# A hybrid decoder step on one core: quarters of weight units between page scores, part of a unit inside the turning of a table, norm sums in pairs

## What is computed

```python
h = rms_norm(x, g_mix)
q, k, v, u, gate_a, gate_s = split(h @ w_in)          # 1024 x 4096
q = rms_norm(q per head, g_q); k = rms_norm(k per head, g_k)
o = stick_breaking_attention(q, k, v)                  # samples also see 2 cached pages of 128 keys
y_ssm, h_last = s5_branch(u, ...)                      # 32 groups, 64 complex states each
ssm_out = (gelu(y_ssm) @ w_glu_val) * sigmoid(gelu(y_ssm) @ w_glu_gate)
x = x + (sigmoid(gate_a) * (o @ w_attn_out) + sigmoid(gate_s) * ssm_out) @ w_out
x = x + square(relu(rms_norm(x, g_mlp) @ w_up)) @ w_down
x = x + (p @ w_ple) * sigmoid(rms_norm(x, g_ple) @ w_ple_gate)
```

## Time and profile before

| | us |
|---|---|
| median of three runs | 948.61 |
| lowest, highest | 947.8, 949.62 |
| the profiled execution, whole | 947.96 |
| its span, first to last instruction | 946.2 |
| PE busy in the span | 922.9 (98%) |
| DVE busy | 610.8 (65%) |
| ACT busy | 439.5 (46%) |
| mean granted TensorE clock | 0.994 of full speed |

### The profile page before, as it was taken

How to read it: one execution, slowest core, us unless ns; L and a number is a source line. 1 busy time by engine, 2 the same in 40 slices (tenths; PEclk the granted TensorE clock), 3 DMA queues, 4 the chain that set the end, 5 groups by cost and what they waited for, 6 DMA issues and landing times.

```text
span 946.2 us, 17809 instructions
## 1 busy us (share of the span) xinstructions
PE 922.9 (98%) x7469; PEld 893.1 (94%) x7469; DVE 610.8 (65%) x855; ACT 439.5 (46%) x672; POOL 66.7 (7%) x115
## 2 busy tenths in 40 slices
PE   5999999999999999999999999999999999999998
PEld 4988999989999878999999999999999999999997
DVE  6399789821477845566567666666676666778453
ACT  7434333221677644445347344444444444445532
POOL 7000031300100310100000000000000000000000
PEclk9999999999999999999999999999999999999999
DMA  8422232822532748432322222322214322252203
GB/s 229 124 67 68 70 106 95 182 83 86 162 97 70 251 156 280 143 105 78 89 68 77 80 90 89 91 89 90 90 47 131 89 89 86 72 159 71 68 1 100
DMA packets 129991, 99.84 MB, mean 106 GB/s; under 512 B 14368, under 2 KB 120216, under 8 KB 129880
## 3 DMA queue, kind: packets, MB, share of 16 engines
q1 hardware_dynamic: 124392, 81.02, 29.1%
q0 software_dynamic: 5424, 17.65, 5.9%
q10 hardware_dynamic: 96, 0.04, 0.0%
HBM read 87.53 MB, written 11.03 MB: 104 GB/s over the span
## 4 chain that ended last, share of the span: by engine, by line
PE 88%; DVE 5%; ACT 4%; issue 2%; DMA 0%; ACTq 0%; DVEq 0%
PE dense L2228 61%; PE banks L2228 20%; PE banks L2381 3%; PE scoreA L2228 3%; PE scoreB L2228 1%; DVE Llo L1679 1%; ACT whi L1259 1%; DVE xtok L1805 1%; ACT t L1561 1%; DVE t L2053 1%; DVE Ssum L1655 0%; DVE mt L1729 0%; DMA xtok<-in_x_sample 0%; ACT ga L1601 0%; PE dense L2381 0%
## 5 line engine op out<-in xcount | busy, mean ns | idle before, releaser
L1679 DVE TENSOR_TENSOR wlo<-wraw,whi 128x1024 fp32r<-128x1024 f32 (+1 forms) x139 | 148.7, 1073 | 102.5 <-ACT whi L1259 90.0
L2228 PE MATMUL dense<-hid,whi 128*128 128x256 f32 (+1 forms) x1024 | 176.6, 294 | 0.1
L2228 PE MATMUL dense<-act_hi,whi 128*128 128x256 f32 (+1 forms) x736 | 169.7, 300 | 2.8 <-ACT act_hi L1413 1.4
L2228 PE MATMUL dense<-act_lo,whi 128*128 128x256 f32 (+1 forms) x736 | 165.7, 295 | 0.0
L2228 PE MATMUL dense<-act_hi,wlo 128*128 128x256 f32 (+1 forms) x736 | 165.4, 295 | 0.0
L2228 PEld LDWEIGHTS dense<-hid,whi 128*128 128x128 f32 x1024 | 152.4, 187 | 0.5 <-issue 0.5
L2228 PEld LDWEIGHTS dense<-act_hi,whi 128*128 128x128 f32 x736 | 125.0, 190 | 7.6 <-issue 3.9
L1259 ACT CAST whi<-wraw 128x1024 fp32r<-128x1024 f32 x100 | 104.9, 1050 | 45.7 <-PE banks L2228 43.8
L2228 PEld LDWEIGHTS dense<-act_lo,whi 128*128 128x128 f32 x736 | 125.9, 190 | 0.0
L2228 PEld LDWEIGHTS dense<-act_hi,wlo 128*128 128x128 f32 x736 | 125.4, 189 | 0.0
L2228 PE MATMUL dense<-hid,wlo 128*128 128x256 f32 (+1 forms) x512 | 108.8, 293 | 0.0
(11 more groups left out here) (368 smaller groups left out, 1574.5 us busy)
## 6 DMA issues: line engine op xcount, KB each, us to landing
wraw<-in_w_in SPq DMA_DIRECT2D x32, 512.0 KB, 4.1
wraw<-in_w_up SPq DMA_DIRECT2D x32, 512.0 KB, 4.1
wraw<-in_w_down SPq DMA_DIRECT2D x32, 512.0 KB, 3.9
gates_spill<-gst POOLq DMA_DIRECT2D x16, 288.0 KB, 2.6
page<-in_cache_k SPq DMA_DIRECT2D x16, 256.0 KB, 8.3
page<-in_cache_v SPq DMA_DIRECT2D x16, 256.0 KB, 7.6
wraw<-in_w_out SPq DMA_DIRECT2D x8, 512.0 KB, 3.7
wraw<-in_w_ple_gate SPq DMA_DIRECT2D x8, 512.0 KB, 3.6
```

The source lines that it names most:

```text
L1679: return nc.vector.tensor_tensor(out=lo, in0=whole, in1=f32(hi), op=ALU.subtract)
L2228: return nc.tensor.matmul(out, lhsT, rhs, start=start, stop=stop, skip_group_check=True)
```

## The change

Four edits, all in the schedule:

1. The norm sums are done two at a time: 0 and 1 after unit 2, 2 and 3 after unit 4, 4 and 5 after unit 6, 6 and 7 after unit 8. Before, one followed each of the units 1 to 8.
2. `turn_back`: between turns 1 and 2 of either table stands the first k step of the next unit (7, and 9): six matmuls, which that unit then no longer has to do.
3. The three half units between the page scores (34's second, both of 35) are cut into quarters of two k steps, 12 matmuls each. Pairs 0, 2 and 4 of pages, which had nothing between transposes and scores, get the first quarter, pairs 1, 3 and 5 the second. Split 37 moves with them, from pair 3 to pair 2.
4. Unit 57 is written as two halves with split 59 between them, where split 59 stood ahead of both.

```diff
+    def half_begin(k1):
+        if halves[0] == 0:
+            flush()
+        event("hpart", n[0], halves[0], k1)
+    def turn_back(part):
+        for i in range(4):
+            if i == 2:
+                event("part", n[0], 0, 1)
+                begun[n[0]] = 1
+            event("gt", part, i, place=2 + i % 2)
...
     unit()
     unit()
+    unit()
     event("qksum", 0)
-    unit()
     event("qksum", 1)
...
-    for i in range(4):
-        event("gt", 0, i, place=2 + i % 2)
+    turn_back(0)
...
-        if i in (1, 3, 5):
-            half_unit()
+        if i in (0, 2, 4):
+            half_begin(2)
+        elif i in (1, 3, 5):
+            half_unit(split_first=False)
...
     event("xsplit", 3)
     event("rscale", 3)
-    unit()
+    half_unit(split_first=False)
+    flush()
+    half_unit()
...
+                elif k == "hpart":
+                    begun[a[0], a[1]] = a[2]
+                    unit(a[0], [a[1]], k1=a[2])
                 elif k == "half":
-                    unit(a[0], [a[1]])
+                    unit(a[0], [a[1]], k0=begun.get((a[0], a[1]), 0))
```

More of the change, by code:

```diff
@@ L259, in schedule_of @@
     unit()
-    event("qksum", 2)
     event("s5in")
     unit()
+    event("qksum", 2)
     event("qksum", 3)
@@ L265, in schedule_of @@
     unit()
-    event("qksum", 4)
     event("s5sq")
     unit()
+    event("qksum", 4)
     event("qksum", 5)
-    for i in range(4):
-        event("gt", 0, i, place=2 + i % 2)
+    turn_back(0)
     event("s5g", 1)
     unit()
-    event("qksum", 6)
     event("s5c", 0)
     unit()
+    event("qksum", 6)
     event("qksum", 7)
-    for i in range(4):
-        event("gt", 1, i, place=2 + i % 2)
+    turn_back(1)
     event("s5c", 1, 0)
```

## The result

The changed kernel takes 940.5 us (median of 5 runs, 938.88 to 942.83), the kernel before, beside it on the same chip, 947.8 (5 runs, 944.8 to 949.62). The ratio is 0.9931, with an interval from 0.9909 to 0.9953.

What follows compares the result with a forecast made beforehand. PE, busy 98% of the span, was taken to bound the kernel. Early part 1.6, page quarters 1.9 and unit 57 1.1 sum to 4.6 us: 948.61 - 4.6 = 944.0 us, range 942.0 to 946.7.

Steps and rivals of the forecast that it cites:

- Sums in pairs: Norm sums after units 2 to 8: joining two visits saves 0.27 us, four times 1.1; bounds nothing to 3.2.
- Turning: Turning of both tables: six matmuls inside save 0.4 us each, 0.8 together; bounds 0.2 and 0.45 each.
- What takes some back: At the first norms PE, 1.9 us earlier, stands 0.2 to 0.4 us for DVE's `nrmr`, ready only some 0.65 earlier.
- the early part: Joined norm sums and table turnings, less PE's stand at the norms: 1.6 us saved, bounds 0.6 and 2.0.
- Quarters: Page scores: a quarter covers the copies in six pairs, 3.18 us each; 1.9 us saved, bounds 0 and 2.2.
- Unit 57: Before unit 58: the earlier addition removes PE's 0.98 us wait and some start-up; 1.1 us saved, bounds 0.9 and 1.2.
- (a): DVE sets the pace from the first norm on, the early part keeps 0.6 us: 945.0 us; chance 0.10.
- (b): Page scores: the quarter does not cover, or the slot's second visit waits for ACT; stage unchanged, 945.9 us; chance 0.03.
- (d): One more clock fall in another pass of y: 947.3 us, no change that could be told; chance 0.07.
- (e): Slower: all four passes of y, moved forward 1.6 us, meet a clock fall, 3.3 us each: 953.9 us; chance 0.04.
- The clock: Pass of y at 208 us: one fall costs 3.3 us; the change only moves the place forward by 1.6 us.
- rival (c): The clock fall at 208 us does not come, 3.3 us less: 940.7 us; chance 0.06.

Runs made afterwards that it cites:

- the third trace of before: The kernel before, unchanged, profiled once more; this run had no fall of the clock and took 945.17 us.
- edit 3 alone: The kernel before with only the quarters of half units between six pairs of pages: median 944.37 us, ratio 0.9982 (0.9964 to 1.0).

## Why the prediction was right in its edits and wrong in its time

**Sums in pairs: mechanism right, 1.1 where 1.36 was measured.** A single sum is 0.60 us from its start to the transposes behind it at 70.65:

```profile
70.05 0.67 PE L2228 MATMUL banks<-gst,hsum 128*16 128x288 f32 x4
```

Two are 1.08 (67.64 to 68.72). So the second costs 0.48, not 0.52, a joined visit saves 0.31 of the 0.79, and four save 1.24. The last 0.1 no row accounts for.

**Turning: mechanism right, 0.8 where 1.14 was measured.** I charged 0.18 us for the visit to dense matmuls and 0.85 for the transposes behind it. The rows of the changed kernel show 0.88 from 69.57 to 70.45, which is 0.09 beyond six matmuls, and 0.79 from 70.45 to 71.24. Two tables: 1.1 by the rows.

**What takes some back: right in kind, 0.3 forecast, 0.27 measured, in part by luck.** PE stands for DVE at the first norm and nowhere after it. But both sides of the meeting were mis-sized: PE came 2.61 earlier there, not 1.9, and DVE's `nrmr` was ready 1.2 earlier (101.02 to 99.81), not 0.65. With the forecast's 0.65 for DVE, PE's 2.61 would have left a stand of about 0.8. The two errors nearly cancel in the stand, in part because the same joined sums and the same turning move both engines. With this the early part gave 2.34 for 1.6, the largest of the mis-sized terms.

**Quarters: 1.9 forecast, 1.88 measured. Unit 57: 1.1 forecast, 1.13 measured.** No other engine had to give anything back, and PE's waits name no new transfer. Rivals (a) and (b) fall with these rows, and (d) and (e) with the clock: neither trace of the changed kernel has a fall in any pass of y.

**The clock is the step that failed.** The sum, 4.6, was set against a trace with a fall and a median of three runs, all of the upper group, and the result taken for a time that keeps the fall: "The change does not touch this place but moves it forward". That is true of the place, but the fall is no property of the kernel. By their times it came in 49 of 86 runs of before and in some 4 of 11 of the changed kernel. About half the runs have it, so the median lies in one group or the other, and the two medians of this result lie in different ones: 947.8 in the upper of before, 940.5 in the lower of after. Lower group against lower group the gain is 5.4 us (5.5 between the traces), and about 1.9 of the 7.3 is which runs made up the medians. Upper against upper it is 6.7 (medians 948.8 and 942.1), but from four runs of the changed kernel, none of them traced. Of the 3.5 us between forecast and result, 0.8 is the size of the edits (5.4 for 4.6), and the other 2.7 is the group: the forecast stood on 948.61, which is 3.5 above the lower group's median, and the result is a run of the lower group that lies 0.8 above its median. I had this as rival (c) with a time of 940.7, 0.2 from the result, and gave it 6 in 100. That it came so near is luck: its edits were 0.8 too small, and 940.5 is the highest run of a group whose median is 939.7. The Trainium skill ("TensorE: Matmul & The Clock Gate", What's actually happening) stood in the prediction with its statement that the chip's look at activity runs freely, and from it I concluded that both kernels meet falls alike. What the runs show is chance in each single run, which makes two groups and not a shared offset. Three runs within 1.8 us looked like a steady state; that three runs all fall in the upper group happens about once in five times (49/86 to the third power).

Whether the changed kernel meets the fall less often (4 of 11 against 49 of 86) can't be told from 11 runs. That its upper runs have their fall at this place was not traced, but it is supported: with the stand taken away in either way, none of its 12 runs lies above 939.6.

**A version that beats both** comes out of the search for the cause: the four edits with the last states out of the way, 938.85 (behind the unit) or 938.93 (bank 2). Against the median of the changed kernel's lower group (939.7) that is 0.8 us less (the stand's 1.24, read in the kernel before, would have given more; where the other 0.4 went stays open), and it has no upper group. It did not run in one comparison with the changed kernel, and the intervals of the ratios overlap (0.9905 to 0.9952 and 0.9887 to 0.993), so this rests on the groups and on the wait that is gone. Against before it is clear, by 0.8 to 0.9% of the time (ratios 0.9909 and 0.9923).

## What to carry over

When runs of a kernel differ by several tenths of a per cent, look at the single times before the median: two groups with nothing between point to an event that comes or not, and a forecast has to say in which group its base and its result lie. A short stand of PE beside small matmuls cost more than its length here: a wait of 0.8 us cost 1.24, and another 3.0 or 4.5 in about half the runs. Such a stand can go without moving any work, by a bank that the next step doesn't write.

## What the runs showed of the hardware

**The fall wants the stand.** All four passes of y are small matmuls. With the stand ahead of pass 2, 49 of 86 runs of before lie in the upper group, without it none of 36 (24 of before, 12 of after). The traced falls took the granted clock to 0.50 for 6.8 and 10.2 us, while PE was busy throughout. The Trainium skill ("TensorE: Matmul & The Clock Gate", A second HAM failure mode: psum-queue depth-cycling) tells of short and frequent idles of PE between groups of matmuls that make the clock go up and down. The runs here are akin to that but not the same case: a single idle of 0.8 us is followed by a single fall, and only in some runs.

**The same dense matmuls run at one of two distances for hundreds in a row.** From 438.14 to 489.73 the trace ahead of the prediction takes 51.59 us, and the third trace of before takes 52.26 for the same work, at full clock both times. The ends of the stretch in the one:

```profile
438.14 0.79 PE L2228 MATMUL dense<-mg,whi 128*128 128x256 f32 x4
...
489.73 1.13 PE L2228 MATMUL banks<-sqsum,ones 128*128 128x288 f32 x4
```

and in the other:

```profile
434.70 0.80 PE L2228 MATMUL dense<-mg,whi 128*128 128x256 f32 x4
...
486.96 1.13 PE L2228 MATMUL banks<-sqsum,ones 128*128 128x288 f32 x4
```

In the first, 395 matmuls follow each other at 130.0 ns on average (256 and 320 columns mixed), in the second at 131.67, and 394 distances x 1.67 ns are 0.66 of the 0.67 us. The changed kernel has 131.67 there. Within this stretch every trace keeps one of the two distances from end to end. The two traces of before with a fall in y have 130.0 here, and of all the others only edit 3 alone has it. It is what gave back part of the fall's price, and it makes differences of half a microsecond between two traces unsafe to explain by an edit. Its cause stays open.
